# Loading an expert's gate and up weights with one 8 MB transfer in place of two of 4 MB, in ten of sixteen turns of a mixture-of-experts layer

## The reference

```python
logits = (x2 @ w_router + b_router).astype(jnp.float32)
top_vals, top_idx = lax.top_k(logits, TOP_K)          # 4 of 32 experts for each token
gates = jax.nn.softmax(top_vals, axis=-1)
...
h = x2[tok] @ w_gu[e] + b_gu[e]                       # w_gu[e]: 1024 x 2048
g = jnp.minimum(h[:, :D_FF], 7.0)
u = jnp.clip(h[:, D_FF:], -7.0, 7.0)
y = (u + 1.0) * (g * jax.nn.sigmoid(1.702 * g))
return y @ w_down[e] + b_down[e]                      # w_down[e]: 1024 x 1024
```

## Time and profile before

| what | value |
|---|---|
| time, median of 3 runs | 1148.26 us (1148.26 to 1148.38) |
| time of the profiled execution | 1146.75 us |
| its span, first to last instruction | 1144.8 us |
| TensorE busy | 1059.2 us, 93% of the span |
| VectorE, ScalarE busy | 442.3 us, 153.9 us |
| SyncE's queue (q1) | 439.86 MB |
| mean granted TensorE clock | 0.968 |

### The profile page before, as it was taken

One profiled execution on the slowest core, in us unless ns is written; L12 is line 12 of the kernel. 1 busy time (PEld: TensorE's weight loads), 2 busy tenths in 40 slices (PEclk: granted clock), 3 DMA queues, 4 the chain that ended last, 5 costly groups with the idle time before them and its releaser, 6 DMA issues.

```text
span 1144.8 us, 20191 instructions
## 1 busy us (share of the span) xinstructions
PE 1059.2 (93%) x8037; PEld 465.0 (41%) x8039; DVE 442.3 (39%) x1311; ACT 153.9 (13%) x334; POOL 59.9 (5%) x38
## 2 busy tenths in 40 slices
PE   9999999998999669999976669999979989999997
PEld 8876559543333213333321213333323333343333
DVE  2767577572533213333321113333313323333324
ACT  2142111230111001111100001111101101111101
POOL 0503370000000000000000000000000000000000
PEclk9999999999999889999987879999999999999999
DMA  9965356989999999999999999999999999999996
GB/s 331 365 233 184 110 189 253 379 324 428 423 433 428 437 430 432 432 429 434 428 437 430 432 433 428 434 428 437 429 433 434 427 433 426 436 428 429 433 425 248
DMA packets 36105, 444.87 MB, mean 389 GB/s; under 512 B 3876, under 2 KB 5160, under 8 KB 21256
## 3 DMA queue, kind: packets, MB, share of 16 engines
q1 hardware_dynamic: 33320, 439.86, 91.2%
q10 hardware_dynamic: 2752, 4.54, 1.3%
HBM read 443.34 MB, written 1.05 MB: 388 GB/s over the span
## 4 chain that ended last, share of the span: by engine, by line
PE 70%; DMA 23%; DVE 3%; another core or an unknown queue 2%; ACT 1%; issue 1%; DVEq 0%; SPq 0%; POOL 0%; POOLq 0%
PE bank L1005 23%; DMA ring<-in_w_down 15%; PE bank L1030 13%; DMA ring<-in_w_gu 8%; PE bank L689 6%; PE bank L981 6%; PE bank L635 5%; PE bank L968 3%; PE bank L814 2%; PE bank L877 2%; PE bank L974 2%; PE bank L1012 1%; PE bank L1018 1%; PE bank L1023 1%; PE bank L999 1%
## 5 line engine op out<-in xcount | busy, mean ns | idle before, releaser
L1005 PE MATMUL bank<-ring,wk 128*32 128x512 f32 x3072 | 369.9, 632 | 63.4 <-DMA ring<-in_w_gu 63.3
L1005 PEld LDWEIGHTS bank<-ring,wk 128*32 128x32 f32 x3072 | 103.9, 116 | 302.4 <-issue 263.8
L1030 PE MATMUL bank<-ring,wk 128*32 128x512 f32 x1632 | 204.8, 600 | 6.2 <-DMA ring<-in_w_down 6.2
L2036 DVE TENSOR_SCALAR wk<-bank 128x256 f32<-128x256 f32 x51 | 21.6, 423 | 461.3 <-PE bank L1005 460.5
L981 PE MATMUL bank<-wk 64*128 64x512 f32 x416 | 103.3, 615 | 2.9 <-ACT wk L1436 2.9
L1030 PEld LDWEIGHTS bank<-ring,wk 128*32 128x32 f32 x1632 | 62.8, 110 | 74.7 <-issue 46.8
L1424 ACT ACTIVATE wk<-wk 128x256 f32<-128x256 f32 x51 | 21.2, 417 | 455.0 <-DVE wk L2036 455.0
L635 PE MATMUL bank<-ring 128*128 128x256 f32 x320 | 70.7, 381 | 0.0
L689 PE MATMUL bank<-ring 128*128 128x512 f32 x152 | 66.4, 593 | 0.0
L981 PEld LDWEIGHTS bank<-wk 64*128 64x128 f32 x416 | 35.8, 186 | 71.4 <-issue 64.0
L635 PEld LDWEIGHTS bank<-ring 128*128 128x128 f32 x320 | 60.2, 190 | 8.9 <-issue 0.8
(11 more groups left out here) (369 smaller groups left out, 881.4 us busy)
## 6 DMA issues: line engine op xcount, KB each, us to landing
ring<-in_w_gu SPq DMA_DIRECT2D x55, 4096.0 KB, 34.8
ring<-in_w_down SPq DMA_DIRECT2D x27, 4096.0 KB, 38.4
ring<-in_w_gu SPq DMA_DIRECT2D x18, 2048.0 KB, 13.4
ring<-in_w_down SPq DMA_DIRECT2D x9, 2048.0 KB, 11.8
ring<-in_w_in SPq DMA_DIRECT2D x4, 2048.0 KB, 19.3
ring<-in_w_ck SPq DMA_DIRECT2D x2, 2048.0 KB, 21.7
ring<-in_w_cv SPq DMA_DIRECT2D x2, 2048.0 KB, 18.0
ring<-in_w_cq SPq DMA_DIRECT2D x2, 2048.0 KB, 8.3
```

The lines of the kernel that those rows point to most:

```text
L1005: ins = mm(hidden(bank, g), rows[:, kk, c, :], half_columns(w[:, kk, :], g), start=False, stop=2 * c + kk == KT - 1, skip_group_check=True)
L1030: ins = mm(strip(7, 2 * d + b), actT[:, b, 2 * c + gg, :], wd[:, gg, b, 512 * d:512 * d + 512], start=c == 0 and gg == 0 and b == 1, stop= ...
```

## The change

For turns 2 to 11 (places 4 to 23) SyncE issues one transfer of 8 MB for all four chunks of gate and up, after all four have been used, and the down weights as before. In HBM an expert's gate and up weights now lie as 64 KB in each of 128 partitions' rows, where they lay as two blocks with 32 KB rows. The slots of `u` = 0 are given out anew so that its four gate and up slots are adjacent. TensorE waits once in a pass, at chunk 0, for the whole transfer. The other turns read the same two halves as before out of the longer rows. Turn 1 is written out of the loop on TensorE, and the counts of the second half's semaphore are lower by the ten turns in which it isn't used (`after`).

```diff
+WHOLE_TURNS = range(2, HEAVY_AT // UNROLL)
-UNIT_SLOT = [6, 4, 0, 8, 10, 2]
-FILL_ORDER = [(0, 2), (0, 0), (0, 1), (0, 4), (0, 5), (0, 3), ...
+UNIT_SLOT = [4, 6, 0, 8, 10, 2]
+FILL_ORDER = [(0, 0), (0, 2), (0, 3), (0, 4), (0, 5), (0, 1), ...
...
+            def load_whole_gate_and_up(e, u, used):
+                at = UNIT_SLOT[u * UNITS_PER_EXPERT] * SLOT
+                for c in range(4):
+                    sp.wait_ge(chunk_used[c], used)
+                sp.nop(nofuse=True)
+                sp.dma_start(ring[:, at:at + 4 * SLOT], w_gu[bass.ds(e, 1)].rearrange("o p n -> (o p) n")).then_inc(unit_landed[u * UNITS_PER_EXPERT], 16)
...
-                    for i in range(UNITS_PER_EXPERT):
+                    if whole:
+                        load_whole_gate_and_up(experts[u], u, passes_till[u])
+                    for i in range(2 if whole else 0, UNITS_PER_EXPERT):
...
-            with sp.Fori(2, LOOPS - 1) as it:
+            with sp.Fori(2, HEAVY_AT // UNROLL) as it:
+                load_later(it * UNROLL, whole=True)
+            with sp.Fori(HEAVY_AT // UNROLL, LOOPS - 1) as it:
                 load_later(it * UNROLL)
...
-                    if c % 2 == 0:
+                    if c % 2 == 0 and not (whole and c == 2):
                         pe.wait_ge(slot_landed[s], 16 * (front_loads[s] + loads))
-                        pe.wait_ge(unit_landed[u * UNITS_PER_EXPERT + c // 2], it * 16 + 16)
+                        pe.wait_ge(unit_landed[u * UNITS_PER_EXPERT + c // 2], own * 16 + 16)
...
-            with pe.Fori(1, heavy_turn) as it:
+            for u in range(UNROLL):
+                all_passes(1, u)
+            with pe.Fori(2, heavy_turn) as it:
                 for u in range(UNROLL):
-                    all_passes(it, u)
+                    all_passes(it, u, whole=True)
...
-"w_gu": lay(w_gu[0].reshape(N_EXP, 2, 2, P, 2, 2 * D_FF).transpose(0, 1, 3, 2, 4, 5).reshape(N_EXP, 2, P, 2 * SLOT))
+"w_gu": lay(w_gu[0].reshape(N_EXP, 2, 2, P, 2, 2 * D_FF).transpose(0, 3, 1, 2, 4, 5).reshape(N_EXP, P, 4 * SLOT))
```

More of the change, by code:

```diff
@@ L69 @@
 HEAVY_AT = RANK_AT.index(UNROLL)
+WHOLE_TURNS = range(2, HEAVY_AT // UNROLL)
 UNITS_PER_EXPERT = EXP_CHUNKS // 2
-UNIT_SLOT = [6, 4, 0, 8, 10, 2]
-FILL_ORDER = [(0, 2), (0, 0), (0, 1), (0, 4), (0, 5), (0, 3), (1, 1), (1, 2), (1, 0), (1, 4), (1, 5), (1, 3)]
+UNIT_SLOT = [4, 6, 0, 8, 10, 2]
+FILL_ORDER = [(0, 0), (0, 2), (0, 3), (0, 4), (0, 5), (0, 1), (1, 1), (1, 2), (1, 0), (1, 4), (1, 5), (1, 3)]
 E_TRI, E_COS, E_SIN, E_NEG, E_POS, E_PAR = 0, 128, 384, 640, 768, 896
@@ L125, in layer_program @@
         lnp = S11[:, half:SLOT]
-        ln3p = S6[:, 0:2 * D]
-        normal_rows, rstd_last = S6[:, 2 * D:3 * D], S6[:, 3 * D:3 * D + P]
+        first_piece = slot_words(UNIT_SLOT[0])
+        ln3p = first_piece[:, 0:2 * D]
+        normal_rows, rstd_last = first_piece[:, 2 * D:3 * D], first_piece[:, 3 * D:3 * D + P]
         aqT = qbuf[:, 0:1024].rearrange("p (m t) -> p m t", m=4)
@@ L430, in load_piece_of_expert @@
             def load_piece_of_expert(e, c):
-                src = w_gu[e, c // 2] if c < 4 else w_down[e]
+                src = w_gu[e, :, (c // 2) * 2 * SLOT:(c // 2) * 2 * SLOT + 2 * SLOT] if c < 4 else w_down[e]
                 landed = unit_landed[e * UNITS_PER_EXPERT + c // 2] if c % 2 else slot_landed[chunk_slot(e, c)]
@@ L465, in load_last_pieces @@
                 at = UNIT_SLOT[UNITS_PER_EXPERT + i]
-                src = w_gu[bass.ds(e, 1), i].rearrange("o p n -> (o p) n") if i < 2 else w_down[bass.ds(e, 1)].rearrange("o p n -> (o p) n")
+                src = w_gu[bass.ds(e, 1)].rearrange("o p n -> (o p) n")[:, i * 2 * SLOT:i * 2 * SLOT + 2 * SLOT] if i < 2 else w_down[bass.ds(e, 1)].rearrange("o p n -> (o p) n")
                 sp.wait_ge(chunk_used[2 * i], used)
@@ L477, in load_last_pieces, with load_later @@
                     sp.dma_start(slot_words(at + 1)[:, half:SLOT], src[:, SLOT + half:2 * SLOT]).then_inc(done, 16)
-            def load_later(e0, ending=False):
+            def load_later(e0, ending=False, whole=False):
                 passes_till = [sp.value_load(cum_i[0:1, bass.ds(e0 + (u - UNROLL), 1)], min_val=1, max_val=MAX_PASSES) for u in range(UNROLL)]
@@ L1043, in _, with expert_pass @@
             open_sum(1, 1)
-            def expert_pass(it, u, loads, ending=False, opening=False):
+            def expert_pass(it, u, loads, ending=False, opening=False, whole=False, after=0):
                 j = pe.snap(passes, min_val=0, max_val=MAX_PASSES)
@@ L1049, in chunk @@
                     s = chunk_slot(u, c)
+                    own = it - after if c // 2 == 1 else it
                     if ending and c >= 2:
@@ L1109, in expert_pass, with two_passes @@
                 pe.reg_add(passes, passes, 1)
-            def two_passes(it, u, loads):
+            def two_passes(it, u, loads, whole=False, after=0):
                 j = pe.snap(passes, min_val=0, max_val=MAX_PASSES)
@@ L1115, in chunk @@
                     s = chunk_slot(u, c)
-                    if c % 2 == 0:
+                    if c % 2 == 0 and not (whole and c == 2):
+                        own = it - after if c == 2 else it
                         pe.wait_ge(slot_landed[s], 16 * (front_loads[s] + loads))
-                        pe.wait_ge(unit_landed[u * UNITS_PER_EXPERT + c // 2], it * 16 + 16)
+                        pe.wait_ge(unit_landed[u * UNITS_PER_EXPERT + c // 2], own * 16 + 16)
                     return slot_words(s)
@@ L1174, in passes_at, with all_passes @@
                 return pe.value_load(npass_i[0:1, place], min_val=least, max_val=SEQ // SLOTS)
-            def all_passes(it, u, ending=False):
+            def all_passes(it, u, ending=False, whole=False, after=0):
                 with pe.Fori(0, passes_at(bass.ds(it * UNROLL + u, 1))):
-                    expert_pass(it, u, 2, ending)
+                    expert_pass(it, u, 2, ending, whole=whole, after=after)
             with pe.Fori(0, passes_of_first):
@@ L1191, in _ @@
                     with pe.Fori(0, passes_at(slice(HEAVY_AT, HEAVY_AT + 1), 2), 2):
-                        two_passes(heavy_turn, u, 2)
+                        two_passes(heavy_turn, u, 2, after=len(WHOLE_TURNS))
                 else:
-                    all_passes(heavy_turn, u)
+                    all_passes(heavy_turn, u, after=len(WHOLE_TURNS))
             with pe.Fori(heavy_turn + 1, LOOPS - 2) as it:
                 for u in range(UNROLL):
-                    all_passes(it, u)
+                    all_passes(it, u, after=len(WHOLE_TURNS))
             pe.wait_ge(shift_landed, 16 * GROUPS)
@@ L1202, in _ @@
             for u in range(UNROLL):
-                all_passes(LOOPS - 2, u)
+                all_passes(LOOPS - 2, u, after=len(WHOLE_TURNS))
             for u in range(UNROLL):
@@ L1208, in _ @@
                             add_rows(t, d)
-                all_passes(LOOPS - 1, u, ending=u == UNROLL - 1)
+                all_passes(LOOPS - 1, u, ending=u == UNROLL - 1, after=len(WHOLE_TURNS))
             total = pe.snap(passes, min_val=1, max_val=MAX_PASSES)
@@ L2171 @@
         "w_cq": lay(w_cq[0]), "w_ck": lay(w_ck[0]), "w_cv": lay(w_cv[0]), "w_co": lay(w_co[0]),
-        "w_router": lay(w_router[0]), "b_router": lay(b_router[0]), "w_gu": lay(w_gu[0].reshape(N_EXP, 2, 2, P, 2, 2 * D_FF).transpose(0, 1, 3, 2, 4, 5).reshape(N_EXP, 2, P, 2 * SLOT)), "b_gu": lay(b_gu[0]),
+        "w_router": lay(w_router[0]), "b_router": lay(b_router[0]), "w_gu": lay(w_gu[0].reshape(N_EXP, 2, 2, P, 2, 2 * D_FF).transpose(0, 3, 1, 2, 4, 5).reshape(N_EXP, P, 4 * SLOT)), "b_gu": lay(b_gu[0]),
         "w_down": lay(w_down[0].reshape(N_EXP, 2, 2, P, 2, D).transpose(0, 3, 1, 2, 4, 5).reshape(N_EXP, P, 2 * SLOT)), "b_down": lay(b_down[0]),
```

2 lines of the change are left out of this document (1 added, 1 removed).

## The result

The changed kernel takes **1157.34 us** (median of 5 runs, 1156.65 to 1157.76), the kernel before 1148.26 (1147.39 to 1149.21): the ratio is **1.008, 95% interval 1.0069 to 1.0091**, 9.1 us slower. The forecast was 1155.4, range 1150.5 to 1162. The profiled execution after took 1157.76 us, 11.0 more than the one before.

The account below looks back on a forecast made before the run. The weight transfer queue was taken as the bound. Idle time of 4.0 and 4.4 us less 1.3 saved made 7.1 us slower: 1153.9 profiled, 1155.4 as median, range 1150.5 to 1162.

Parts of the forecast that it names:

- What bounds the kernel: Weight queue: time is the sum of all transfers plus time the DMA queue stands empty; TensorE is not the limit overall.
- Fewer transfers: Twenty pairs become twenty single transfers in a full queue: 0.06 us saved each, 1.3 us in all, bound 0.
- each transfer pays its start-up: Rival, 3%: every transfer pays the 2.4 us start-up, so 48 us would be saved, giving 1108.7 us.
- A later issue: In turns 2 to 11 the 8 MB wait for chunk 3, taking 3.43 us of queue at each issue.
- lateness behind a long wait: TensorE restarts on all 64 matmuls at lowered clock, losing 2.4 us: 3.3 us late from place 7, 3.15 from 16.
- The rival in which the lateness does not build up: Rival, 9%: TensorE's clock returns at once and other waits absorb the rest: +0.6 us, 1148.9, no change.
- The rival in which the clock stays low for all 64 matmuls: Rival, 7%: the long wait costs 6.9 us over all 64 matmuls: +20.2 us, 1168.5.
- What an empty queue costs: At thin issues the engines idle by 2.4 us of start-up less the work left in the queue.
- The sum: Idle 4.0 us up to 511.54, 4.4 at 803.42, 0 at 889.33, less 1.3 saved: 7.1 us slower.
- The wait for 8 MB at place 9: Not an added cost: the transfer lands at 480.8, and TensorE comes to it at 481.5.
- Turn 1 written out: Turn 1 outside TensorE's loop, one of the items the prediction put at nothing.
- The layout read more slowly: Rival, 7%: the new layout reads slower, 3.9 us per per cent; at 3.3% 12.8 us more, 1168.2.

Follow-up runs that it names:

- the longer program: The changed kernel with turns 3, 8 and 11 also written outside TensorE's loop, without extra matmuls: 1160.80 us, ratio 1.0107 to the kernel before.
- the layout alone: New memory layout, new slots and turn 1 written out, with transfers and waits as in the kernel before: 1148.76 us, ratio 1.0003 to that kernel.
- late start: New layout and slots, two 4 MB transfers issued early as before; TensorE waits for both before chunk 0 in turns 2 to 11: 1152.77 us, ratio 1.0037.
- late issue: New layout and slots, two 4 MB transfers both issued after chunk 3 in turns 2 to 11; TensorE starts on the first half: 1152.92 us, ratio 1.0048.

## Why the prediction was right, and by how much it was off

**What bounds the kernel.** Right. The last weights land 11.1 us later and the profiled execution is 11.0 longer, so all of the loss is in the queue of weights. TensorE's waits grew without costing anything by themselves: with turns 6 and 7 whole it had three waits of 12.0 to 12.6 us, and the four thin places lost nothing.

**Fewer transfers.** 1.3 us was forecast, 0.06 a pair; the landings give 19.43 - 19.35 = 0.08 a pair, 1.6, and the rows were not cut. That each transfer pays its start-up is refuted by the same figure.

**A later issue, and lateness behind a long wait.** Right, both shown alone and together, and the second by holding the clock up. Place 7's down products started at 433.79, 4.47 later than before; the landing that released it came 421.22 - 419.61 = 1.61 later, so TensorE's own lateness was 2.9, for 3.3 forecast. At place 16, 699.78 - 691.56 - (686.97 - 681.85) = 3.1, for 3.15. The rival in which the lateness does not build up has no ground: the issue for place 9 is 8.2 us later, 3.4 of it for chunk 3 and 1.6 for the later landing, and the rest is lateness. The rival in which the clock stays low for all 64 matmuls would have needed 13.7 us for them; 8.39 to 9.51 were seen.

**What an empty queue costs.** 2.4 us was taken from one 2 MB transfer; the three issues show 2.5. That it is 2.5 less what is left holds within 0.2 where the queue is dry: -0.2, -0.5, -1.0, -1.9, -2.4, -2.5 and -2.6 left cost 2.7, 3.0, 3.3, 4.5, 4.8, 5.0 and 5.2 in the runs above (the longer program had one more, -0.6 for 4.2, with a fetch of code in the same transfer). With 1 to 4 us left it is loose: between nothing and 2.8 us. For this forecast that did little harm, as two of the three issues found a dry queue.

**The sum.** Up to the second issue 4.0 forecast, 4.2 measured; at place 21 4.4, measured 5.0; at place 24 0, measured 0. With the saving of 1.6 the predicted terms come to 7.6, for 7.1. The wait for 8 MB at place 9 did not come on top, though barely: the transfer landed at 460.41 + 21.9 = 482.3, and TensorE came to it at 482.70 with no wait.

**What it left out.** The medians differ by 9.1, 1.5 over these terms, and the two profiles by 11.1 at the last weights. What has no term in the prediction is the fetching of code. "Turn 1 written out" stood at nothing; it makes 27 fetches for 25. In the time that does not show, as the layout alone has the same 27 and the ratio 1.0003. In this one profile the rest of the loss stands in single steps, most of them at fetches. At place 4 a transfer lost 1.0 us with 4.9 left (8.2 before, less the 3.43 of the later issue), a place that the prediction did not list. Its issue at 308.71, and the stretch from 331 to 333, just ahead of its landing at 334.0, in the DMA view of the changed kernel:

```profile
ring<-in_w_gu SPq DMA_DIRECT2D x1, 25.3
...
q8 instruction: 1, 0.02, 3.0%
```

Whether the fetch or the thinner queue took this 1.0 is not shown. With turns 8 to 11 whole, the transfer issued there at 304.41 found 8.2 left as before and had its fetch at 314.2 as before, and landed after 18.9 us for 17.9. So a fetch can do it, and need not. Two more steps, of 1.3 to 1.4 us near 935 and 1044, lie at fetches too; the kernel before has one of 1.5 near 965. Another 1.0 us of the 11.1 was there before the first changed transfer, a difference of the two profiled executions. 7.6 + 1.0 + 1.0 + (1.36 + 1.26 - 1.54) = 10.7 of 11.1. The layout, the third thing put at nothing, cost nothing.

**Rivals.** The layout read more slowly: refuted (19.35 us, and the layout alone 1.0003). The Trainium skill's fit of about 2.0 us for each transfer issued from GpSimd, in DMA: Bandwidth & Descriptors, section Anatomy of one DMA, would have given an estimated 40 us; these queued transfers of SyncE show 0.08 for one transfer saved, and a price of that size, 2.5, only where the queue was dry.

**Not settled.** Why a queue with 1 to 4 us left costs nothing at one issue and 2 us at another of the same size (late start: 2.5 left cost 2.0; late issue: 2.6 left cost 0.3). One part the traces show: the sixteen engines do not finish together, so "left" is that of the slowest. In the changed kernel the last transfer ahead of place 9's issue landed at 459.9, and in the late-issue run at 457.67 + 2.6 = 460.2, but the stretches ahead of that were far from full already (columns as above; a packet counts where it starts):

```profile
457.00:459.00 2.00, 2.00 (x24) 0.54 (x20) 0.00 (x0) 0.00 (x0) 0.00 (x0) 1.00 0.23 98
```

```profile
456.00:458.00 2.00, 2.00 (x20) 0.62 (x10) 0.59 (x2) 0.14 (x1) 0.00 (x0) 1.00 0.50 213
```

Yet the second of these lost only 0.3 us. What decides between 0.3 and 2.0 stays open, as does which fetches of code cost time.

## What to carry to other kernels

When a stream of transfers is the bound, look for the issues with the least work ahead of them, and price an edit by what it takes from that margin: a merged transfer that is issued later and waited for as a whole spends it twice, once at the issue and once in the engine that uses the data. The saving per transfer in a full queue has to be read from two landings and the issues between them; here it was a thirtieth of the start-up that a lone transfer shows. And code written out of a loop is loaded by the same DMA engines: count its fetches before calling it free. Here two more could not be seen in the time, and eleven more could.

## What the runs showed of the hardware

- An 8 MB transfer in rows of 64 KB takes 19.35 us in a full queue, two of 4 MB 19.43; behind a dry queue both pay 2.3 to 2.7 us once, beside the time for which it was dry.
- The sixteen engines do not finish a transfer together: their share was 0.23 in the 2 us that ended 0.9 us ahead of a last landing.
- A fetch of 16 KB of program code holds one DMA engine for 1.0 us; eleven more of them made a kernel bound by its weight queue 4.5 us slower, ratio 1.0047 (1.0033 to 1.0061), though 18 of 23 showed 0.3 us or nothing.
- After waits of 11.6 to 13.7 us 64 matmuls took 8.4 to 9.5 us for 7.05, a loss of 1.3 to 2.5 us; the granted clock just behind the wait at place 7 was at the lower level, 0.50. Products that nothing uses, done in that wait, kept it at 1.00.
